# Eight places of tile 0's second block without a gather turn, and tile 1's residual and norm steps moved behind them

## The reference

```
# first block, its second half
h2 = modulate(rms_norm(x, g_ffn), sh2, sc2)
# product-key routing: 8 heads, 16 experts each of 16384, for every token
x  = x + gt2 * sum_{128 rows (h,k)} gate * gelu(h2 . peer_u[e]) * peer_v[e]
x  = rms_norm(x, g_final)
# second block
h = rms_norm(x, norm_mix_g);  proj = h @ w_in                  # 1024 x 7168
y_a = gelu(za_u) * (tril(W_s) layer_norm(gelu(za_v)) + b)      # spatial gating
y_b = causal attention, 16 heads, with a bias by distance
x = x + (sigmoid(g_a) * y_a + sigmoid(g_b) * y_b) @ w_out
x = x + relu(rms_norm(x, norm_ffn_g) @ w_ff1)**2 @ w_ff2       # 1024 x 4096 x 1024
x = x + sigmoid(rms_norm(x, norm_ple_g) @ w_ple_gate) * (p @ w_ple_proj)
out = rms_norm(x, norm_final_g)
```

## Time and profile before

| | us |
|---|---|
| median of 3 runs | 1434.87 (1433.56 to 1436.04) |
| profiled execution, own time | 1433.82 |
| its span | 1432.0 |
| TensorE busy (PE) | 1303.1, 91% of the span |
| VectorE busy | 779.4, 54% |
| ScalarE busy | 330.7, 23% |
| transfers | 517.86 MB, mean 362 GB/s |

### The profile page before, as it was taken

How to read it: one execution, slowest core, us unless ns; L and a number is a source line. 1 busy time by engine, 2 the same in 40 slices (tenths; PEclk the granted TensorE clock), 3 DMA queues, 4 the chain that set the end, 5 groups by cost and what they waited for, 6 DMA issues and landing times.

```text
span 1432.0 us, 14639 instructions
## 1 busy us (share of the span) xinstructions
PE 1303.1 (91%) x4872; PEld 745.1 (52%) x4872; DVE 779.4 (54%) x2085; ACT 330.7 (23%) x867; POOL 304.1 (21%) x275
## 2 busy tenths in 40 slices
PE   7999999999999888779888989798886899999998
PEld 7777996565565554434344544344332344544444
DVE  4356536687677766777766557565656532210002
ACT  2231224322221132232221312111110133411102
POOL 0000002343433332434222323232333000000000
PEclk7999999999999998999999999999999999999999
DMA  9966886999999999999999999999999899678883
GB/s 389 406 218 248 313 281 244 417 418 419 414 418 417 418 406 408 408 377 396 417 416 416 367 415 388 414 384 415 417 417 416 331 412 374 218 249 284 286 299 116
DMA packets 101305, 517.86 MB, mean 362 GB/s; under 512 B 11632, under 2 KB 12528, under 8 KB 66416
## 3 DMA queue, kind: packets, MB, share of 16 engines
q0 software_dynamic: 38592, 293.62, 50.0%
q1 hardware_dynamic: 61344, 219.38, 41.2%
q10 hardware_dynamic: 1296, 3.93, 0.7%
HBM read 515.84 MB, written 1.05 MB: 361 GB/s over the span
## 4 chain that ended last, share of the span: by engine, by line
PE 37%; DMA 17%; DVE 1%; ACT 1%; issue 0%; ACTq 0%; DVEq 0%
PE ps_M L954 26%; DMA ring<-in_w_second 14%; DMA ring<-in_w_pq 3%; PE ps_T L749 3%; PE ps_T L750 3%; PE ps_SA L718 1%; PE ps_OT L942 1%; PE ps_SA L1011 1%; PE ps_T L942 1%; PE ps_M L970 0%; PE ps_S L983 0%; PE ps_SA L1023 0%; DVE hT L2253 0%; DVE ring L2042 0%; ACT arena L1566 0%
## 5 line engine op out<-in xcount | busy, mean ns | idle before, releaser
L954 PE MATMUL ps_M<-ring,arena 128*128 128x512 f32 x1072 | 491.2, 599 | 41.4 <-DMA ring<-in_w_second 40.8
L954 PEld LDWEIGHTS ps_M<-ring,arena 128*128 128x128 f32 x1072 | 194.0, 190 | 284.7 <-issue 229.3
L1250 POOL DMA_INDIRECT ring<-in_peer_uv,arena x137 | 158.6, 1158 | 327.4 <-PE ps_T L750 299.7
L1250 POOL DMA_INDIRECT arena<-in_peer_uv,arena x105 | 121.0, 1152 | 317.7 <-PE ps_T L750 231.3
L749 PE MATMUL ps_T<-ring,arena 128*128 128x512 f32 x230 | 125.6, 629 | 24.3 <-ACT arena L1386 24.3
L1375 ACT ACTIVATE arena<-arena 128x2 f32<-128x2 f32 x128 | 25.9, 202 | 427.7 <-DVE arena L2062 427.2
L750 PE MATMUL ps_T<-ring,arena 128*128 128x512 f32 x230 | 121.9, 612 | 0.0
L2042 DVE SCALAR_TENSOR_TENSOR ring<-ring,merged 128x1024 f32<-128x1024 f32 x73 | 89.0, 1221 | 49.3 <-DMA ring<-in_peer_uv,arena 49.2
L749 PE MATMUL ps_T<-arena 128*128 128x512 f32 x178 | 94.2, 611 | 17.1 <-ACT arena L1386 17.1
L2042 DVE SCALAR_TENSOR_TENSOR ring<-ring,arena 128x1024 f32<-128x1024 f32 x64 | 77.8, 1219 | 29.2 <-DMA ring<-in_peer_uv,arena 28.8
L750 PE MATMUL ps_T<-arena 128*128 128x512 f32 x178 | 91.8, 598 | 0.0
(11 more groups left out here) (304 smaller groups left out, 1541.4 us busy)
## 6 DMA issues: line engine op xcount, KB each, us to landing
ring<-in_w_second SPq DMA_DIRECT2D x274, 512.0 KB, 8.5
ring<-in_w_in SPq DMA_DIRECT2D x70, 512.0 KB, 7.8
arena<-in_w_ada POOLq DMA_DIRECT2D x12, 2048.0 KB, 11.2
ring<-in_w_pq SPq DMA_DIRECT2D x30, 512.0 KB, 10.3
ring<-in_w_out SPq DMA_DIRECT2D x16, 512.0 KB, 7.1
ring<-in_w_br SPq DMA_DIRECT2D x16, 384.0 KB, 7.6
ring<-in_peer_uv,arena POOLq DMA_INDIRECT x137, 13.0
arena<-in_rel SPq DMA_DIRECT2D x1, 2048.0 KB, 16.4
```

The costliest lines, as they stand in the source:

```text
L954: m = mm(bank, left[c], w[:, c, :], start=first and c == 0, stop=last and c == 1)
L1250: pool.indirect_dma_start(row_slots[s], None, A["peer_uv"], bass.IndirectOffsetOnAxis(ap=expert[:, u % 3, k:k + 1], axis=0))\
```

## The change

The test `has_turn` is replaced by a table `TURN_AT`, which gives each place its turn or none. Of the first 128 places those with number 15, 31, 47, 63, 79, 95, 111 and 127 have none, so every later turn comes one place later for each of them, and turn 256 stands at place 136, behind quarter 128. Rows, tiles, slots and all instructions are the same in number. `FIRST` is built from the same table, so the query tiles move with their turns. Tile 1's residual and norm steps stand later: `residual(1)` is split, its products at (27, 0) and its sum at (27, 1) behind x6's second half, `middle_sum(1)` at (27, 1), `normed(1)` at (27, 2), `fourth_sum(1)` at (27, 3), the x4 transposes at (27, 3) and (28, 0), `both_turned` at (28, 1) ahead of `ple_add(0, 0)`.

```diff
-def has_turn(n):
-    return n <= NH * TOPK
+SPREAD = 8
+TURN_AT, turn_here = [], 0
+for n in range(LEAD + QUARTERS):
+    if turn_here > NH * TOPK or n % 16 == 15 and n // 16 < SPREAD:
+        TURN_AT.append(None)
+    else:
+        TURN_AT.append(turn_here)
+        turn_here += 1
...
-    if has_turn(n):
+    if TURN_AT[n] is not None:
...
-                elif at in ((26, 12), (26, 13)) and t == 0:
-                    half = q - 12
+                elif at in ((27, 3), (28, 0)) and t == 0:
+                    half = w - 27
                     pe.wait_ge(x_mid, 2)
                     turn(1, ("x4", 1, half), halves(x_tok[:, 1, :], half))
...
-                place = next(places)
-                n = NH * TOPK + place
-                if place < NH * TOPK:
+                turn_here = TURN_AT[next(places)]
+                if turn_here is None:
+                    return
+                n = NH * TOPK + turn_here
+                if turn_here < NH * TOPK:
                     beside(n // TOPK - 1, n % TOPK)
...
-                elif at == (26, 10) and t == 0:
+                elif at == (27, 1) and t == 0:
                     middle_sum(1)
-                elif at == (26, 12) and t == 0:
+                elif at == (27, 3) and t == 0:
                     fourth_sum(1)
...
                     half_turned("x6", t, 1, h_b, "norm_ple_g_2")
+                    if t == 0:
+                        residual_sum(1)
...
-                elif at == (26, 9) and t == 0:
-                    residual(1)
-                elif at == (26, 11) and t == 0:
+                elif at == (27, 0) and t == 0:
+                    residual_product(1)
+                elif at == (27, 2) and t == 0:
                     normed(1)
-                elif at == (26, 14) and t == 0:
-                    both_turned("x4", 1, h_a, "norm_mix_g_2")
                 elif at == (28, 1):
+                    if t == 0:
+                        both_turned("x4", 1, h_a, "norm_mix_g_2")
                     ple_add(t, 0)
```

22 lines of the change are left out of this document (13 added, 9 removed).

## The result

The changed kernel takes 1427.75 us (median of 5, 1426.84 to 1428.1); before took 1435.45 us beside it (median of 5, 1433.56 to 1439.3). The ratio is 0.994, 95% interval [0.992, 0.9959]: faster by 0.6%, between 5.9 and 11.5 us.

A forecast was written before the change was run, and what follows sets the result against it. Queues bound the kernel up to the last row, TensorE after it. -13.73 + 10.96 + 0.1 = -2.7 us gave 1431.1 us from the profile, 1432.2 us from the median; range 1428.7 to 1437.3 us.

The forecast's parts named there:

- What bounds the kernel: Whole kernel: queues limit until the last row, TensorE after it; eight quarters leave the TensorE regime, saving 13.73 us.
- The steps of tile 1 and SP's queue: Behind the last row: later tile 1 steps add 0.1 us; SP's waits for row slots cost nothing, with 2.2 us slack.
- Gathers end later by 6 x 1.254 + 2 x 1.717 = 10.96 us: Ahead of the last row: eight added tiles, six priced at queue time and two at TensorE time, lengthen the gather phase.
- the prices: Per exchanged place: one weight tile costs 1.254 us of queue time, one quarter behind the last row saves 1.717 us.
- Pricing two places at 1.717: At 870 to 885 and 930 to 945 us, TensorE's work was taken to count, so each place costs 1.717 us.
- Idle queue is recovered: Gather phase: shifted turns part heavy places; a third of 10 us idle queue returns, 1428.9 us; chance 18%.
- Slower: tiles outnumber rows: Gather phase: extra tiles beside queries idle the queues 0.83 us each, 2.9 us slower, 1437.8 us; chance 17%.
- No gain: Gather phase: queues not full often enough, so places exchange one for one at 1.717 us, 1434.9 us; chance 22%.
- The test that the forecast set itself: Gather phase: GB/s stays at 408; under 402 speaks for more tiles than rows, over 412 for recovered idle queue.
- its four cases: End of the last row's passes: 1145.4 us forecast, 1144.4 queues full, 1148.1 one-for-one exchange, 1151 tiles outnumbering rows.

The follow-up runs named there:

- e1: The changed kernel with no place left without a turn, so only tile 1's residual, norm and x4 steps stand late; 1436.0 us, ratio 0.9996 to before.
- e5: The changed kernel with only places 15 and 31 without a turn instead of eight; 1427.92 us, ratio 0.9940 to before.
- e7: The kernel before, all turns in place, with the later phases' query tiles and their copies one turn later; 1431.74 us, ratio 0.9961.
- e8: The kernel before, all turns in place, with VectorE's row step ahead of its block step in both tiles; 1430.92 us, ratio 0.9953.
- e2: The changed kernel with its eight places without a turn at 89, 94, 99 and so on to 124, behind the last query; 1435.08 us, ratio 0.9995 to before.
- e15: The kernel before, with VectorE's row step ahead of its block step only at tile 0's three long waits; 1431.26 us, ratio 0.9977.

## Why the prediction was wrong

**What bounds the kernel: right.** Two regimes, and one work item moved from one to the other. A quarter is worth 1.717 us of tail: 297.7 to 284.0 us for eight, 290.8 for four, 294.3 for two.

**The steps of tile 1 and SP's queue: right.** x_mid at 9.7 us for 9.6 forecast, no wait for w0 132, x4 or w1 4, and e1 shows the moved steps to be worth nothing by themselves, within 2.7 us.

**"Gathers end later by 6 x 1.254 + 2 x 1.717 = 10.96 us": the step that failed.** The stretch grew by 7.8 us, 3.2 less. Three things in the term were wrong, and by the two profiles they make up the difference:

- Two of the eight places were priced at 1.717 instead of 1.254 us: 0.9 us.
- Eight tiles were put ahead of the last row. SP has seven more out by then, w0 131 for w0 124, because w0 132 stands for row 255's slot; the prediction has this hold in its part on SP's queue and did not carry it into the sum. Seven tiles are 8.8 us, not 10.03: 1.25 us.
- The idle queue time of before was taken to stay as it is. The remaining 1.0 us is idle time that came back. It is the difference of two larger parts: in 660 to 1110 us, 410 GB/s for 407 means about 3 us less idle time (10.5 to 7.5 against 417 GB/s), and behind 1110 us, 350 GB/s in 32.2 us for 365 in 24.35 means about 2 us more, at the dry end shown above.

That pair understates what the medians show. The profiles differ by 5.7 us: 13.6 of tail less 8.8 for seven tiles is 4.8, and 1.0 has come back. The medians differ by 7.7 us (8.2 between the means of the five runs each, 1435.84 and 1427.64). Against e1, which is before's order up to the last row and whose profile lies at its median, the idle time falls by 3.8 us (16.4 to 12.6). So the recovered idle time is 1 to 4 us, and its size is not known better. That there is such a recovery does not rest on this pair: e5 gains 8.6 us (0.6% of 1436.86) with only two places exchanged, 0.9 by the prices, and e7 and e8 gain 5 to 7 with none.

**Pricing two places at 1.717 because TensorE was full there was a mistake of its own.** At 870 to 885 us TensorE was busy 15.00 of 15 us at 379 GB/s; I took this for a place where TensorE's work counts. TensorE is still at 15.00 there in the changed kernel at 418 GB/s, and in e1, in before's order, at 410: a full TensorE does not go with idle queues there. That it works off a backlog from the query and the piece 20 us earlier fits, but no run isolates it.

**The rivals.** "Idle queue is recovered" was the right mechanism, at 18%. Its size, a third of 10 us, is about that of the recovery up to 1110 us. That its time of 1428.9 comes near 1427.75 is in part luck: the third was picked and not worked out, and the count of tiles and the dry end, off to either side, partly cancel. I wrote that nothing in before says which way the meeting of pieces and turns goes. That was wrong: VectorE's brackets of 8.21, 8.82 and 8.73 us stood in before's timeline, each behind a query half on TensorE, and the order of the changed kernel could have been laid beside them: at all three sites the piece comes ahead of the query half it stood behind. That would have named the sites, not the size. "Slower: tiles outnumber rows" would have shown under 402 GB/s; it was 410. "No gain" is refuted for the change, but e2's median is near it. The test that the forecast set itself did not decide as it said: 410 lies between its bounds of 402 and 412, and the last row came at 1142.20, below all of its four cases.

**What stays open.** How much of the gain belongs to each of the three sites; why the first dip outlives VectorE's wait in e8 and e15 (the late passes at the lower clock are there in both, but no run takes the clock away alone) and yet e8 gains 5 to 7 us; and what a late place is worth, by the medians something between nothing and 0.4 us. The change of the median by one site is 1 to 3 us, at the border of what these runs part.

## What to carry to other kernels

When an edit shifts one sequence against another, the price of what is moved is only half of the sum: lay the two orders side by side at the longest waits of the in-order engines, and see whether the pairs that met there still meet. A stretch where one engine is full and the transfers dip is not proof that the engine bounds it: look for the same stretch in another order, and at the waits ahead of it. When a term counts transfers ahead of a mark, count in the issue list which ones leave ahead of it. And before taking a large edit as the cause of its gain, do its first quarter alone; here two places out of eight did all of it, and three moved steps on VectorE some 40% (3.3 us, interval 1.0 to 5.6, of 8).

## What the runs showed of the hardware

A single weight tile that comes late holds not only its own matmuls but all rows behind them: the query half waited 1.89 us, and the gathers stood 9.4 and 10.6 us apart instead of 3.76. In the stretches around such a place the queues move 417 GB/s (660 to 780 and 1000 to 1125 us), and in no slice of the two pages over 420, so that what they idle there is not made up.

TensorE's granted clock fell at one of the stalls: 0.57 from 786 to 790 us, behind 1.89 us of idle time, and two passes of 512 columns took 1.91 us for 1.02. The waits of 1.86 and 1.87 us at the other two sites, ahead of the queries at 850.70 and 915.81, were not followed by it; their passes took 1.02.

The scatter of one kernel is larger than that of a profile's parts: the tail of 284.0 to 284.6 us agrees within 0.6 us over six kernels with eight places, while the start of tile 0's second block over all kernels moves between 653.4 and 657.1 us and the phase over the kernels with eight places between 487.0 and 492.3. A median over many executions and a cut of the profile at fixed marks answer different questions, and both were needed.
